# Scaling attention probabilities ahead of their transposes, in a two-block transformer kernel

## The reference

```
p = softmax(s)                      # over the keys; a sink adds exp(sink) to the sum
o = einsum('bhqk,bkhd->bqhd', p, v)
```

## Time and profile before

| | |
|---|---|
| median of three runs | 1763.15 us |
| span of the profiled execution | 1760.3 us, first to last instruction |
| TensorE busy | 1686.9 us, 96% |
| VectorE busy | 1096.3 us, 62% |
| ScalarE busy | 834.9 us, 47% |
| attention of layer 0 | about 126 to 239 us |
| attentions of layers 2 and 3 | about 1149 to 1185 and 1496 to 1532 us |

### The profile page before, as it was taken

The page is one execution under the profiler, slowest core; times in us unless marked ns, Lnnn a source line. Parts: engine busy times, 40 slices in busy tenths (PEclk is TensorE's granted clock), DMA queues, the critical chain, the costliest instruction groups (busy, mean ns, idle before and its releaser), DMA issues.

```text
span 1760.3 us, 30030 instructions
## 1 busy us (share of the span) xinstructions
PE 1686.9 (96%) x11624; PEld 1458.1 (83%) x11624; DVE 1096.3 (62%) x2108; ACT 834.9 (47%) x1540; POOL 85.1 (5%) x90
## 2 busy tenths in 40 slices
PE   3999999999999999998999999999999999999998
PEld 1995577888888879985799998968999998689998
DVE  4436655634343444358776676767878757678786
ACT  4237754423232333236454454575645546755453
POOL 2100011000000012110100001001000000000000
PEclk9999999999999999999999999999999999999999
DMA  9628664333333333336556663614666536146662
GB/s 293 180 69 259 226 192 108 108 96 96 96 98 95 106 109 108 101 128 205 143 166 182 183 177 95 190 34 119 184 182 196 150 100 191 33 136 178 184 200 87
DMA packets 406252, 254.43 MB, mean 145 GB/s; under 512 B 8448, under 2 KB 405024, under 8 KB 406112
## 3 DMA queue, kind: packets, MB, share of 16 engines
q1 hardware_dynamic: 404576, 248.80, 48.2%
q0 software_dynamic: 1536, 3.71, 0.8%
HBM read 251.36 MB, written 1.11 MB: 143 GB/s over the span
## 4 chain that ended last, share of the span: by engine, by line
PE 86%; DVE 7%; ACT 3%; issue 2%; DMA 1%; SPq 0%; DVEq 0%; ACTq 0%
PE bank L2173 57%; PE bank L2190 15%; PE bank L2434 3%; PE bank L2314 2%; PE bank L2445 2%; PE bank L2455 2%; PE bank L2152 2%; DVE parts L1135 1%; PE bank L2200 1%; PE bank L2429 1%; ACT parts L1319 1%; PE bank L2461 1%; DMA H<-ctx_t 1%; PE bank L2470 1%; ACT PR L1510 1%
## 5 line engine op out<-in xcount | busy, mean ns | idle before, releaser
L2173 PE MATMUL bank<-AT,parts 128*128 128x256 f32 (+2 forms) x4128 | 604.0, 308 | 9.7 <-DVE parts L1135 2.9
L2173 PEld LDWEIGHTS bank<-AT,parts 128*128 128x128 f32 (+1 forms) x4128 | 561.1, 190 | 51.8 <-issue 9.8
L1135 DVE TENSOR_TENSOR parts<-raw,parts 128x1024 fp32r<-128x1024 f32 (+1 forms) x368 | 440.1, 1216 | 137.7 <-ACT parts L1319 136.7
L1319 ACT ACTIVATE parts<-raw 128x1024 fp32r<-128x1024 f32 (+1 forms) x368 | 372.8, 1042 | 296.7 <-PE bank L2173 167.2
L2173 PE MATMUL bank<-parts,AT 128*128 128x256 f32 x2112 | 259.0, 284 | 4.0 <-DVE WORK L1961 2.0
L2173 PEld LDWEIGHTS bank<-parts,AT 128*128 128x128 f32 x2112 | 256.0, 192 | 5.5 <-DVE WORK L1961 2.5
L2190 PE MATMUL bank<-HID,parts 128*128 128x256 f32 (+1 forms) x1216 | 215.8, 338 | 3.1 <-DVE HID L1817 3.1
L2190 PEld LDWEIGHTS bank<-HID,parts 128*128 128x128 f32 x1216 | 185.3, 188 | 31.4 <-DVE HID L1817 4.8
L2173 PE MATMUL bank<-HID,parts 128*128 128x512 f32 x768 | 175.4, 390 | 0.0
L2173 PEld LDWEIGHTS bank<-HID,parts 128*128 128x128 f32 x768 | 144.1, 188 | 30.3 <-issue 0.5
L2053 DVE SCALAR_TENSOR_TENSOR H<-bank,MOD,H 128x256 f32<-128x256 f32 x160 | 73.6, 481 | 122.1 <-PE bank L2173 111.6
(11 more groups left out here) (201 smaller groups left out, 1501.1 us busy)
## 6 DMA issues: line engine op xcount, KB each, us to landing
raw<-mlp_w SPq DMA_DIRECT2D x128, 512.0 KB, 4.2
raw<-ada_w SPq DMA_DIRECT2D x96, 512.0 KB, 4.9
raw<-w_up SPq DMA_DIRECT2D x88, 512.0 KB, 4.6
raw<-w_in SPq DMA_DIRECT2D x32, 512.0 KB, 4.7
raw<-w_down SPq DMA_DIRECT2D x32, 512.0 KB, 4.6
raw<-odd_w_in SPq DMA_DIRECT2D x24, 512.0 KB, 4.0
raw<-w_out SPq DMA_DIRECT2D x16, 512.0 KB, 4.7
raw<-even_w_in SPq DMA_DIRECT2D x12, 512.0 KB, 6.5
```

The lines of the kernel that those rows point to most:

```text
L1135: ng.tensor_tensor(chunk_part(c, 1), chunk_raw(c), chunk_part(c, 0).bitcast(F32), ALU.subtract)\
L1319: return nc.scalar.activation(o, i, ACT.Copy)
L2173: ins = MM(out, stay, move, start=opens and kt == 0 and i == 0, stop=kt == kts - 1 and i == 2 and stops)
```

## The change

Between the scores of step i and the turn of step i-2 a unit `scale` for step i-1 is added to the list. In it VectorE waits for the exponentials of both jobs, adds the sinks where there are any, takes the reciprocals of the two sums, and multiplies the two tiles of probabilities in place by their column. TensorE's turn of a job waits for its product (`p_scaled`) in place of the exponentials. The reciprocals spread by TensorE, their copy, the multiplication of the output, the reciprocals of fours and the buffers `OUT` and `ROOTS` are dropped. ScalarE rounds the output to its high part straight from PSUM, and VectorE subtracts for the low part in the same unit; `flush` stays in the list and does nothing. The unit takes no bank.

```diff
             for j in steps[i] if i < n else ():
                 for m in range(j.get("maps", 1)):
                     add("score", ("score", j["j"], m), map=m, job=j)
+            if size == 2 and 0 <= i - 1 < n:
+                add("scale", ("scale", steps[i - 1][0]["j"]), job=steps[i - 1][0], four=steps[i - 1])
+                index[("scale", steps[i - 1][1]["j"])] = units[-1]
...
                 if layer == 1:
                     consumed(pe, index[("turn_o", layer, kt // 2)].u)
                 else:
-                    pe.wait_ge(head_low, fours_done(layer, kt))
+                    consumed(pe, four_done(layer, kt))
...
-                elif k == "value" and x.four or k == "flush":
-                    if k == "value":
-                        filled(act, x.u)
-                        copy(ROOTS[:, x.c % 2, :], b[:, N:2 * N]).then_inc(root_turned, 1)
-                    if k == "flush" or x.job["j"] != first_four[x.job["layer"]]:
-
-                        y = last_four[x.layer] if k == "flush" else fours[x.c - 1]
-                        consumed(act, y.u)
-                        copy(four_to(y, 0), OUT[:, y.c % 4, :]).then_inc(head_high, 1)
+                elif k == "value" and x.four:
+                    filled(act, x.u)
+                    copy(four_to(x, 0), b[:, 0:N]).then_inc(head_high, 1)
...
-                elif k == "turn_p" and x.job["kind"] != "D":
-                    y = x.job["of"]
-                    if x.four[-1] is y.four[-1]:
-                        for j in y.four:
-                            consumed(dve, index[("score", j["j"], 0)].u)
-                        i, to = roots(y)
-                        den = DEN[:, i:i + 4]
-                        if y.job["kind"] in ("A", "CA"):
-                            step(V.tensor_tensor(ES[:, i:i + 4], ES[:, i:i + 4], den, ALU.add))
-                            settle()
-                            den = ES[:, i:i + 4]
-                        V.reciprocal(to, den).then_inc(root_ready, 1)
-                elif k == "value" and x.four or k == "flush":
-                    if k == "value":
-                        filled(dve, x.u)
-                        dve.wait_ge(root_turned, x.c + 1)
-                        V.tensor_tensor(OUT[:, x.c % 4, :], b[:, 0:N], ROOTS[:, x.c % 2, :], ALU.mult).then_inc(drained, 1)
...
+                elif k == "scale":
+
+                    for j in x.four:
+                        consumed(dve, index[("score", j["j"], 0)].u)
+                    i = x.st.nm % 8
+                    den = DEN[:, i:i + 2]
+                    if x.job["kind"] in ("A", "CA"):
+                        step(V.tensor_tensor(ES[:, i:i + 2], ES[:, i:i + 2], den, ALU.add))
+                        settle()
+                        den = ES[:, i:i + 2]
+                    step(V.reciprocal(RD[:, i:i + 2], den))
+                    settle()
+                    for m in range(2):
+                        p = PR[:, (x.st.nm + m) % 4, 0:x.job["keys"]]
+                        V.tensor_scalar(p, p, RD[:, i + m:i + m + 1], None, ALU.mult).then_inc(p_scaled, 1)
+                elif k == "value" and x.four:
+                    filled(dve, x.u)
+                    dve.wait_ge(head_high, x.c + 1)
+                    V.tensor_tensor(four_to(x, 1), b[:, 0:N], four_to(x, 0).bitcast(F32), ALU.subtract)\
+                        .then_inc(drained, 1)
...
-                            consumed(pe, s.u)
+                            y = index[("scale", j["j"])]
+                            pe.wait_ge(p_scaled, 2 * y.i + y.four.index(j) + 1)
...
-                    pe.wait_ge(root_ready, x.c + 1)
-                    for v in range(TB):
-                        for i in range(2):
-                            r = roots(x)[1][:, 2 * v + i:2 * v + i + 1].broadcast_to([P, HD])
-                            last = MM(bank[HD * i:HD * i + HD, x.u % BANKS, N + v * P:N + v * P + P], r, order_of(x.job), start=True,
-                                      stop=True, tile_position=(0, HD * i))
```

More of the change, by code:

```diff
@@ L479, in plan @@
     count = dict(mod=0, square=0, scaled=0, hid=0, rot=0, rope=0, post=0, conv=0, comb=0, sumsq=0, mid=0, rstd=0, nm=0,
-                 statn=0, sums=0, relu=0, ada_row=0, ada=0, ada_group=0)
+                 statn=0, sums=0, relu=0, scale=0, ada_row=0, ada=0, ada_group=0)
     chunks, of_panel = [], []
@@ L495, in plan @@
     for pos, x in enumerate(units):
-        if x.kind not in ("ada_row", "ahead", "post", "tail", "apply", "mix", "soft", "flush", "prep", "rstd", "final", "near"):
+        if x.kind not in ("ada_row", "ahead", "post", "tail", "apply", "mix", "soft", "scale", "flush", "prep", "rstd", "final", "near"):
             x.u = u
@@ L541, in plan @@
             count["conv"] += 1
+        if x.kind == "scale":
+            x.st = index[("score", x.job["j"], 0)]
+            x.i = count["scale"]
+            count["scale"] += 1
         if x.kind == "mix":
@@ L681, in two_block_kernel @@
         out_high = sem("out_high")
-        root_ready = sem("root_ready")
-        root_turned = sem("root_turned")
+        p_scaled = sem("p_scaled")
         head_high = sem("head_high")
-        head_low = sem("head_low")
         columns_in = sem("columns_in")
@@ L773, in two_block_kernel @@
         KQ = WORK[:, 0:4, :].rearrange("p a t -> p (a t)")
-        OUT = WORK[:, 4:6, :].rearrange("p a (b t) -> p (a b) t", t=N)
-        ROOTS = WORK[:, 6, :].rearrange("p (b t) -> p b t", t=N)
         PT0 = TOK[:, 6144:10240].rearrange("p (s x) -> p s x", s=2)
@@ L992, in turned_pair @@
             return slot[:, (i * (j["keys"] // P) + t) * N:(i * (j["keys"] // P) + t + 1) * N]
-        def roots(x):
-            i = index[("score", x.job["j"], 0)].nm % 8
-            return i, RD[:, i:i + 4]
         def four_to(x, part):
@@ L1004, in four_to, with four_done @@
             return AT[:, part, ft, lo:lo + N]
-        def fours_done(layer, ft):
-            return max(x.c for x in fours if x.layer_of == layer and x.ft_of == ft) + 1
+        def four_done(layer, ft):
+            return [x for x in fours if x.layer_of == layer and x.ft_of == ft][-1].u
         def turned_o_to(x):
@@ L2454, in _ @@
                         for i in range(2):
-                            MM(bank[HD * i:HD * i + HD, x.u % BANKS, 0:N], values_of(x.four[i])[t], turned_pair(x, i, t),
-                               start=t == 0, stop=t == tiles - 1, tile_position=(0, HD * i))
-                    pe.wait_ge(root_ready, x.c + 1)
-                    for v in range(TB):
-                        for i in range(2):
-                            r = roots(x)[1][:, 2 * v + i:2 * v + i + 1].broadcast_to([P, HD])
-                            last = MM(bank[HD * i:HD * i + HD, x.u % BANKS, N + v * P:N + v * P + P], r, order_of(x.job), start=True,
-                                      stop=True, tile_position=(0, HD * i))
+                            last = MM(bank[HD * i:HD * i + HD, x.u % BANKS, 0:N], values_of(x.four[i])[t],
+                                      turned_pair(x, i, t), start=t == 0, stop=t == tiles - 1, tile_position=(0, HD * i))
                 elif k == "value":
```

## The result

The changed kernel takes 1776.45 us (median of four runs, 1775.78 to 1777.47) beside 1763.68 for the kernel before on the same chip: a ratio of 1.0076, interval 1.0062 to 1.0089. It is slower by 13 us, where 9.7 were forecast; the direction and the range held, the size was short by 3.

A forecast was written before the change was run, and what follows sets the result against it. TensorE was taken to set the first layer's pace, a VectorE-ScalarE loop that of the third and fourth. 1763.15 + 9.7 (9.2 later layers, 0.5 first) = 1772.8 us; own range 1767 to 1778, 8 in 10 from 1757 to 1781.

The forecast's parts named there:

- The rival in which VectorE's scale comes in time: Faster rival: first layer keeps its whole 9.6 us, third and fourth lose 2.3 each; 1758.2 us, chance 0.17.
- 0.35 and 0.48 forecast: VectorE's in-place product of probabilities by a column: 0.35 us for 256 columns, 0.48 for 512.
- One column a cycle: Rival: VectorE's products take 0.48 and 0.75 us, lengthening rounds and pairs of heads; 1781 us, chance 0.10.
- First layer, forecast +0.5: First layer's attention, eight pairs of heads: 9.6 us saved, 10.1 lost, 0.5 net loss.
- The lateness: First layer: TensorE's turn of the latent step waits for its scale, once per pair of heads; 10.1 us lost.
- 16 times 0.60 is 9.6: First layer: 16 output products each lose spreading matmuls worth 0.60 us of TensorE's stream, saving 9.6 us.
- The bound for this term: First layer's best case: no lateness of the turns, so 9.6 us gained; the worst case was +4.
- 1.16 and 1.36 with sinks: First layer: the latent turn's lateness per pair, 1.16 us in four pairs and 1.36 in the four with sinks.
- Fourth layer, forecast +4.6: Fourth layer's attentions: 2.0 us for five longer rounds, 2.2 for three scales at the start, 0.4 at the end.
- 4.85: Third and fourth layers: one round of the VectorE and ScalarE loop takes 4.85 us against 4.31.
- Third layer, forecast +4.6: Third layer's attentions: same terms as the fourth's, 2.0, 2.2 and 0.4 us; 9.2 for the two layers.
- a rival with 0.07 and three stretches of 1.5 us: Clock rival: TensorE's clock falls behind each of three attentions, 1.5 us each; 1777.3 us, chance 0.07.

## Why the prediction was right, and where it was short

**The mechanism.** The turn waits for a product that stands behind the maxima in VectorE's queue: shown by the waits in the trace, by the same work without the wait (18.6 us less by the medians, 2.3 of them the clock in the third layer), and by the product put ahead of or behind the real ones. The rival in which VectorE's scale comes in time is out.

**The price of a product.** 0.35 and 0.48 forecast, 351 and 494 ns measured. One column a cycle is out.

**First layer, forecast +0.5, measured +3.24.** The lateness was priced at 10.1 and costs 9.4. VectorE's work, priced at nothing, costs 0.34. The step that failed is the other term, "16 times 0.60 is 9.6": the removal brings 6.5. I took the distance between two starts in the last layer's stream for what the first layer's would lose; without the narrow matmuls the stream behind an output product starts 0.2 later than it did behind them. The bound for this term had been 9.6 as the best case, and no row was read for what follows the product once the spreading is gone. Also the waits are not the two sizes of the forecast, 1.16 and 1.36 with sinks. The first two pairs wait 2.0 us each: less of TensorE's stream lies ahead of the turn there (no other transposes in the first, a sum of 0.38 in place of rows of the modulation in the second), and the one pair that I read has both. The other pairs wait 0.9 to 1.2, with or without sinks, and a ninth wait, of 1.4, stands behind the last pair. They add up to 12.1, of which the stage loses 9.4.

**Fourth layer, forecast +4.6, measured +4.14.** The rounds of the second attention are 4.77 and not 4.85, those of the first 4.92. (The sum had 4.87 a round where its own working gives 4.85, which is 0.1 a layer.) The first transposes of the third layer come 7.07 us after the first score product, against 5.56 before: 1.5 later, as written. What the end of the attention costs was not measured by itself.

**Third layer, forecast +4.6, measured +7.14.** 2.3 are the clock, which had been a rival with 0.07 and three stretches of 1.5 us; the forecast itself put the clock at nothing. One fall was worth 2.3, not 1.5. Another, ahead of the first turn of the fourth layer (0.55 from 1506 to 1508), cost nothing: it lengthened idle transposes behind which the turn then no longer waited, and the first turn came 7.06 us after the first score product, as in the third layer. The Trainium skill (TensorE: Matmul & The Clock Gate, part 1) takes the clock away after an idle window. I had read from it that these waits were too short for that, which gave 1772.8; the trace shows the fall with no wait for another engine over 1.91 us, so here the measurement decides against my use of the rule.

**The sum.** 3.1 too much gain from the removal, 2.3 for the clock and 0.3 for VectorE's work in the first layer, less 0.7 for the turn's lateness there, 0.2 in what else the later layers cost and 0.8 outside the attentions: 3.1 + 2.3 + 0.3 - 0.7 - 0.2 - 0.8 = 4.0, and the span is 13.7 longer where 9.7 were forecast. The two large misses add up, so the range did not hold because errors cancelled.

## What to carry to other kernels

Before an operation is moved from behind a result to ahead of its first use, ask which queue it stands in and what stands ahead of it: the work itself cost 7 us here (1750.6 to 1757.9), and the wait for it 18.6 more, 2.3 us of clock in the third layer included. Giving its user one step more, with two more buffers, took back the 13 us that the change had cost. Moving the operation forward in its own queue made it worse; by the waits it then held back what another engine was waiting for. Look at the granted clock of each stage before a difference is put down to the order of work: it fell in several of these kernels where the waits had grown. And price a removal in a dense stream by what follows it, from the start of the work that stays to the start of the next, not by the length of the piece that goes.

## What was not expected of the hardware

A product of 128 by 256 fp32 by a column takes 925 ns on GpSimd and 351 on VectorE, 2.6 times as long. The Trainium skill (GPSIMD Engine Reference, section 4.1) calls elementwise work with one input roughly line-rate there; at 925 ns for 256 columns, 3.6 ns a column, that isn't seen in this trace. Only this width was run, so what one instruction costs by itself is in that figure. While GpSimd ran four of them, VectorE's maxima beside them kept their 0.42 us.

The granted clock fell to 0.50 in the third layer behind 3 us in which TensorE was busy for 1.16, and did not at the same place of the fourth layer, where TensorE was busy for 1.16 too and the last turn waits as long (1.91). What the two differ in was not found.
